# Attention's in-projection as seven block products over the whole contraction, with its weights' forms in three buffers

## What is computed

```python
def _dilated_attention_mixer(h, w_in, w_out):
    bsz, s, _ = h.shape
    proj = h @ w_in                       # (1024, 1024) @ (1024, 10240)
    qkv = proj[..., :N_DIL * 3 * A_WIDTH].reshape(bsz, s, N_DIL, 3, A_HEADS, A_HEAD_DIM)
    gate = proj[..., N_DIL * 3 * A_WIDTH:]
    for g, (window, dil) in enumerate(((128, 1), (512, 4), (2048, 16))):
        o, l = _dilated_group(qkv[:, :, g, 0], qkv[:, :, g, 1], qkv[:, :, g, 2], window, dil, slopes)
    wts = softmax(stack(lses, axis=-1))   # over the three groups
    o = einsum('bshg,bshgd->bshd', wts, stack(outs, axis=3))
    y = o.reshape(bsz, s, A_WIDTH) * silu(gate)
    return y @ w_out
```

## Time and profile before

| | |
|---|---|
| median of three runs | 2149.3 us |
| the profiled execution | 2158.68 us, span 2156.9 us |
| PE busy | 2034.0 us (94%), 10859 matmuls |
| DVE | 1306.4 us (61%) |
| ACT | 1003.0 us (47%) |
| POOL | 1062.9 us (49%) |
| DMA | 229.41 MB, 106 GB/s |
| attention's pairs | about 137 to 1154 us |

### The profile page before, as it was taken

One profiled execution on the slowest core, in us unless ns is written; L12 is line 12 of the kernel. 1 busy time (PEld: TensorE's weight loads), 2 busy tenths in 40 slices (PEclk: granted clock), 3 DMA queues, 4 the chain that ended last, 5 costly groups with the idle time before them and its releaser, 6 DMA issues.

```text
span 2156.9 us, 33831 instructions
## 1 busy us (share of the span) xinstructions
PE 2034.0 (94%) x10859; PEld 1619.4 (75%) x10859; DVE 1306.4 (61%) x2731; ACT 1003.0 (47%) x2441; POOL 1062.9 (49%) x710
## 2 busy tenths in 40 slices
PE   5799999999999999999998989899999998998997
PEld 4578787787877878878786777677777776776886
DVE  5655546446455465554555576697498498487553
ACT  3334444444434444344445245674575475485320
POOL 1533463363543635436345174475366365386572
PEclk9889999999999999999999999999999999999999
DMA  8322131221221312203024332555355355367431
GB/s 286 107 60 79 42 99 48 60 89 39 71 78 41 107 39 68 81 22 114 34 70 157 112 130 55 158 166 162 99 166 153 100 175 137 102 199 229 164 117 39
DMA packets 118408, 229.41 MB, mean 106 GB/s; under 512 B 21376, under 2 KB 64000, under 8 KB 118272
## 3 DMA queue, kind: packets, MB, share of 16 engines
q1 hardware_dynamic: 118272, 227.84, 34.3%
HBM read 199.42 MB, written 28.39 MB: 106 GB/s over the span
## 4 chain that ended last, share of the span: by engine, by line
PE 66%; DVE 13%; issue 6%; ACT 5%; DMA 4%; POOL 4%; SPq 1%; DVEq 0%; ACTq 0%; POOLq 0%
PE pp L673 18%; PE po L673 16%; PE pp_s L2369 7%; PE sp_ L750 4%; PE tp L760 3%; PE yo_p L2573 3%; DMA w_raw_s<-in_b_w 2%; DVE stage_s L2999 2%; PE po L833 2%; PE pp_s L2573 2%; DVE vv L2935 2%; PE st_p L2573 1%; PE fill L2573 1%; PE po L822 1%; ACT prob L1083 1%
## 5 line engine op out<-in xcount | busy, mean ns | idle before, releaser
L673 PE MATMUL pp<-h_forms,w_hi 128*128 128x512 f32 x1094 | 342.2, 394 | 0.0
L2369 PE MATMUL pp_s<-h_hi,w_hi_s 128*128 128x512 f32 x624 | 269.9, 433 | 22.2 <-DVE stage_s L2999 14.6
L556 POOL TENSOR_TENSOR w_lo<-w_raw,w_hi 128x1024 fp32r<-128x1024 f32 x76 | 182.8, 2406 | 218.4 <-ACT w_hi L1032 218.1
L2369 PE MATMUL pp_s<-h_hi,w_lo_s 128*128 128x512 f32 x624 | 245.9, 394 | 0.0
L2369 PE MATMUL pp_s<-h_lo,w_hi_s 128*128 128x512 f32 x624 | 245.5, 393 | 0.0
L673 PE MATMUL po<-h_forms,w_hi 128*128 128x512 f32 x760 | 238.0, 395 | 6.2 <-ACT gate L1032 6.2
L1083 ACT ACTIVATE prob<-prob,mz 128x256 f32<-128x256 f32 (+2 forms) x384 | 169.3, 442 | 140.2 <-DVE mz L1326 140.1
L673 PEld LDWEIGHTS pp<-h_forms,w_hi 128*128 128x128 f32 x1094 | 203.2, 189 | 41.0 <-ACT vT L1032 0.3
L673 PE MATMUL pp<-h_forms,w_lo 128*128 128x512 f32 x546 | 213.5, 391 | 0.0
L1346 DVE COPY probT<-tp 128x512 f32<-128x512 f32 x160 | 103.3, 684 | 134.8 <-PE tp L760 134.8
L673 PEld LDWEIGHTS po<-h_forms,w_hi 128*128 128x128 f32 x760 | 143.2, 190 | 39.9 <-ACT gate L1032 9.2
(11 more groups left out here) (524 smaller groups left out, 4594.0 us busy)
## 6 DMA issues: line engine op xcount, KB each, us to landing
w_raw<-in_a_w SPq DMA_DIRECT2D x80, 512.0 KB, 4.1
rw<-cum_rows SPq DMA_DIRECT2D x32, 1024.0 KB, 6.2
w_raw_s<-in_b_w SPq DMA_DIRECT2D x40, 512.0 KB, 3.9
ew<-exp_rows SPq DMA_DIRECT2D x64, 256.0 KB, 7.2
num_wide<-in_ada_w SPq DMA_DIRECT2D x16, 768.0 KB, 6.1
num_wide<-merge_rows SPq DMA_DIRECT2D x16, 768.0 KB, 7.8
num_wide<-in_ada_w SPq DMA_DIRECT2D x20, 512.0 KB, 6.2
yT_b<-trunk SPq DMA_DIRECT2D x32, 256.0 KB, 2.4
```

Source lines behind the costliest of these rows:

```text
L556: return nc.gpsimd.tensor_tensor(out, x, hi.bitcast(F32), ALU.subtract)
L673: last = nc.tensor.matmul(bank, w, h, start=begin and i == 0, stop=end and i == 2)
L2369: last = nc.tensor.matmul(out, w[:, slot, k, :], of_h(h, k, half), start=(k == 0 and n == 0), stop=(k == KT - 1 and n == 2))
```

## The change

All eight k tiles of every unit go through the seven products: KS is 4, PL and `plain` are gone, and so are the plainly made first tiles. A unit has seven forms of weights (B11, B21, three sums in buffers of their own, two sums in place), each of 512 elements per partition, and each form has a high and a low part in one of three buffers, `w_f[:, SLOTS[i]]`; the raw sum lies where the low part will. Forms 0, 3 and 5 share a buffer, 1 and 4, 2 and 6. h is held only in its seven forms. The first four k-tile blocks of unit 0's first three products run as h is made (`beginning`). Two units stand ahead of the pairs, every pair has five in a new order, the last pair three (d = 0 to 5). The transposes of v stand at d = 0, 3 and 8, behind the values. Buffers of the merge shrink: group 2's share is loaded when POOL has added group 1's (`third_share`), and ada_w's rows of the next layer come one by one through a ring of three, in their own pair (`NEXT_AT`), none at the start. ACT's steps are `even_step` and `odd_step`.

```diff
-KS = 2
-PL = KT - 2 * KS
+KS = KT // 2
 A11, A12, A22, S1, S2, S3, S4 = range(7)
-DUOS_OF_TILES = ((VT2, Q2), (K2, VT0), (Q0, K0), (GATE, VT1), (Q1, K1))
-LAST_DUOS = ((VT2, Q2), (K2, GATE))
-FIRST_DUO = (Q1, K1)
-PLAIN = 4
-NT_UNITS = 1 + 5 * (PAIRS - 1) + 2
-EVENTS, SUMS = 9, 9
+FIRST_DUOS = ((Q0, K0), (VT0, Q1))
+DUOS_OF_TILES = ((K1, VT1), (Q0, K2), (Q2, VT2), (K0, GATE), (VT0, Q1))
+LAST_DUOS = ((K1, VT1), (Q2, K2), (GATE, VT2))
+AHEAD = (Q0, K0, VT0, Q1)
+FIRST_UNITS = len(FIRST_DUOS)
+NT_UNITS = FIRST_UNITS + 5 * (PAIRS - 1) + len(LAST_DUOS)
+EVENTS, SUMS, FORMS = 7, 8, 7
...
+        SLOTS = (0, 1, 2, 0, 1, 0, 2)
+        PRODUCTS = (A11, A12, S3, S2, A22, S1, S4)
...
-        V_AT = {2: 2, 4: 0, 8: 1}
+        V_AT = {0: 0, 3: 1, 8: 2}
...
                 with sp.Fori(0, PAIRS - 1) as j:
-                    load_unit(5 * j + 3)
-                    store_y(j)
-                    sp.wait_ge(y_sent, 16 * j + 16)
-                    load_next(j + 1)
-                    for i in range(4, 7):
-                        load_unit(5 * j + i)
+                    n = 5 * j + 4
+                    until_next_rows(j)
+                    load_x_tile(n + 1)
+                    load_y_tile(n + 1)
+                    load_next(j, range(3, 6))
+                    load_x_tile(n + 2)
+                    load_next(j, range(6, KT))
+                    load_y_tile(n + 2)
+                    load_x_tile(n + 3)
                     stats(j, T_AT)
-                    load_unit(5 * j + 7)
+                    load_y_tile(n + 3)
                     weights_out(j)
+                    load_x_tile(n + 4)
+                    load_y_tile(n + 4)
+                    third_share(j)
...
+                def low_part(n, i, x):
+
+                    hi, lo = (w_f[:, SLOTS[i], s] for s in range(2))
+                    pool.wait_ge(w_rounded, FORMS * n + (i + 1))
+                    rest(lo, x, hi).then_inc(w_ready, 1)
+
+                def raw_form(i):
+                    return w_f_raw[:, SLOTS[i], 1]
+
+                def early_forms(n):
+
+                    first = isinstance(n, int) and n == 0
+                    low_part(n, 0, B11)
+                    low_part(n, 1, B21)
+                    pool.wait_ge(w_in[1], 16 * n + 16)
+                    if not first:
+                        pool.wait_ge(pp_full, EVENTS * n)
+                    nc.gpsimd.tensor_tensor(raw_form(2), B22, B12, ALU.subtract).then_inc(t_made, 1)
+                    pool.wait_ge(t_made, 3 * n + 1)
+                    nc.gpsimd.tensor_tensor(B12, B12, B11, ALU.subtract).then_inc(p_step, 1)
+                    low_part(n, 2, raw_form(2))
+
+                def middle_forms(n):
+
+                    pool.wait_ge(p_step, 1 if isinstance(n, int) and n == 0 else 12 + 2 * n + 1)
+                    pool.wait_ge(pp_full, EVENTS * n + 1)
+                    nc.gpsimd.tensor_tensor(raw_form(3), B22, B12, ALU.subtract).then_inc(t_made, 1)
+                    low_part(n, 3, raw_form(3))
+                    pool.wait_ge(w_ready, FORMS * n + 2)
+                    nc.gpsimd.tensor_tensor(B21, B21, B22, ALU.subtract).then_inc(p_step, 1)
+                    pool.wait_ge(p_step, 12 + 2 * n + 2)
+                    pool.wait_ge(pp_full, EVENTS * n + 2)
+                    nc.gpsimd.tensor_tensor(raw_form(4), B21, B12, ALU.add).then_inc(t_made, 1)
+                    low_part(n, 4, raw_form(4))
...
+                    n = 5 * j + 7
+                    forms(n)
+                    weigh(j, 0)
+                    weigh(j, 1)
+                    add_share(j, 1)
+                    n = 5 * j + 8
+                    early_forms(n)
+                    middle_forms(n)
+                    weigh(j, 2)
+                    low_part(n, 5, B12)
+                    add_share(j, 2)
+                    low_part(n, 6, B22)
+                    gated_sum(j)
...
+                def product(n, i, bank, blocks=range(KS)):
+
+                    (w1, w2), (h1, h2) = ([w_f[:, SLOTS[i], s] for s in range(2)],
+                                          [h[:, PRODUCTS[i]] for h in hs])
+                    for b in blocks:
+                        for t, (w, h) in enumerate(((w1, h1), (w1, h2), (w2, h1))):
+                            last = nc.tensor.matmul(bank, w[:, b], h[:, b], start=b == 0 and t == 0,
+                                                    stop=b == KS - 1 and t == 2)
+                    if blocks[-1] == KS - 1:
+                        last.then_inc(pp_full, 1)
...
                 def first_half(n):
 
-                    first = isinstance(n, int) and n == 0
-                    pe.wait_ge(w_ready, 4 * n + 1)
-                    pe.wait_ge(pp_free, PP_FREE + 4 * n - 1)
-                    product(b0, rows_of(0, B_X), A11, begin=True, end=True).then_inc(pp_full, 1)
-                    if first:
-                        pe.wait_ge(pp_free, PP_FREE)
-                    product(b1, rows_of(0, B_Y), A12, begin=True)
-                    plain(b1, 0, 0, end=True).then_inc(pp_full, 1)
-                    pe.wait_ge(w_ready, 4 * n + 2)
-                    pe.wait_ge(pp_free, PP_FREE + 4 * n)
-                    if first:
-                        pe.wait_ge(h_lo, KT + 1)
-                    product(b2, T2, S2, begin=True, end=True).then_inc(pp_full, 1)
+                    pe.wait_ge(w_ready, FORMS * n + 1)
+                    pe.wait_ge(pp_free, 4 * n - 2)
+                    product(n, 0, b0)
+                    pe.wait_ge(w_ready, FORMS * n + 2)
+                    pe.wait_ge(pp_free, 4 * n - 1)
+                    product(n, 1, b1)
+                    pe.wait_ge(w_ready, FORMS * n + 3)
+                    pe.wait_ge(pp_free, 4 * n)
+                    product(n, 2, b2)
+                    fourth_product(n)
+
+                def fourth_product(n):
+
+                    pe.wait_ge(w_ready, FORMS * n + 4)
                     pe.wait_ge(comb, SUMS * n + 1)
-                    if first:
-                        pe.wait_ge(h_lo, KT + 2)
-                    product(b0, T3, S3, begin=True, end=True).then_inc(pp_full, 1)
+                    product(n, 3, b0)
+
+                def second_half(n, between=None):
+
+                    pe.wait_ge(w_ready, FORMS * n + 5)
                     pe.wait_ge(comb, SUMS * n + 3)
-                    plain(b2, 0, 1, begin=True).then_inc(pp_full, 1)
-
-                def second_half(n, between=None):
-
-                    pe.wait_ge(w_ready, 4 * n + 4)
-                    product(b2, T4, A22, end=True).then_inc(pp_full, 1)
-                    pe.wait_ge(pp_free, PP_FREE + 4 * n + 1)
-                    if isinstance(n, int) and n == 0:
-                        pe.wait_ge(h_lo, KT + 4)
-                    product(b1, rows_of(1, B_X), S1, begin=True, end=True).then_inc(pp_full, 1)
-                    pe.wait_ge(comb, SUMS * n + 4)
-                    plain(b0, 1, 1, begin=True, end=True).then_inc(pp_full, 1)
+                    product(n, 4, b0)
+                    pe.wait_ge(w_ready, FORMS * n + 6)
+                    pe.wait_ge(pp_free, 4 * n + 1)
+                    product(n, 5, b1)
                     if between:
                         between()
-                    pe.wait_ge(pp_free, PP_FREE + 4 * n + 2)
-                    product(b2, rows_of(1, B_Y), S4, begin=True)
-                    plain(b2, 1, 0, end=True).then_inc(pp_full, 1)
+                    pe.wait_ge(w_ready, FORMS * n + 7)
+                    pe.wait_ge(comb, SUMS * n + 4)
+                    product(n, 6, b2)
...
+                pair_sums(0)
+                for i in range(KS):
+                    beginning(i, (0, 1))
+                    if i + 1 < KS:
+                        pair_sums(i + 1)
+                    beginning(i, (2,))
+                pe.wait_ge(h_lo, FORMS * KS - 1)
+                fourth_product(0)
+                pe.wait_ge(h_lo, FORMS * KS)
+                second_half(0)
+                first_half(1)
                 scores(0, 0)
-                second_half(0)
+                second_half(1)
...
-                FIRST_TILE_AT = {6: (0, 1), 7: (2, 3), 8: (4, 5, 6)}
+                FIRST_TILE_AT = {8: (0, 1, 2), 9: (3, 4, 5, 6)}
...
                 def stretch(j, d, table):
 
                     if d:
-                        new_v(j, d - 1, table)
                         duo_values(j, d - 1, table)
+                    new_v(j, d, table)
                     if d < DUOS - 1:
                         scores(j, d + 1)
                     new_probs(j, d, table)
...
+                def even_step(j, n, kinds, before, numerators_of, softmax_of):
+
+                    second_tile(j if before[1] != Q1 else j - 1, n - 1, before, 0)
+                    numerators_of()
+                    round_form(n, 2)
+                    softmax_of()
+                    round_form(n, 3)
+                    first_tile(j, n, kinds, 0)
+                    round_form(n, 4)
+
```

(47 more changed lines are left out.)

882 lines of the change are left out of this document (374 added, 508 removed).

## The result

The changed kernel takes 2163.4 us (median of four runs, 2162.0 to 2165.8), the kernel before 2149.2: a ratio of 1.0069, 95% interval 1.0051 to 1.0086. The forecast was 2105 us with a range of 2084 to 2127, so it missed by 58 us and had the wrong sign. Two runs of later experiments, of 5572 and 3330 us, lie far from the others of their kernels and are left out of the ratios.

A forecast was written before the change was run, and what follows sets the result against it. TensorE's matmul count was taken to bound the pairs, other engines being in time. Terms -31.3 + 6.2 - 6.2 + 11 - 22 - 2 = -44.3 us gave 2105 us from 2149.3, range 2084 to 2127.

The forecast's parts named there:

- Part 1: Pairs: 138 fewer matmuls at 0.227 us, -31.3 us; two more attention stretches +6.2, gate tile's wait gone -6.2.
- Part 2: Pairs: POOL, ACT and DVE bring weight forms, sums and evacuations in time despite more work; cost nothing.
- (c): Rival, pairs: fourth product late in every unit, its rounding queued behind ACT's softmaxes; 2.1 us per unit, +84, 2189 us; chance 0.05.
- Part 3: Start of each next pair: prob's transposes wait for DVE behind the shares, 1.6 us a pair, +11 us; bounds 0 and 3.
- Part 4: Start, before the loop: two units replace four plain tiles and one unit; loop begins at 115 us, -22; bounds 108 and 137.
- Part 5: End, last product to second output tile: about 36 us for 38.5, w_out's blocks through two slots; -2, bounds -9 and +4.
- The sum's carrying over to the median: Whole kernel: unprofiled median 9.4 us below the profiled execution; same difference assumed after the change, 2149.3 - 44.3 = 2105 us.
- row against rule: Start: DVE subtraction took 3.37 us beside POOL, 1.23 otherwise, agreeing that two-SBUF-input DVE and GpSimd instructions block; 22 us in full, 5 held.

The follow-up runs named there:

- the numerators in place: Changed kernel with DVE's copies first, shares behind the next duo's score maxima, and ACT copying a pair's first numerators ahead of its softmax: 2115.6 us, ratio 0.9842.
- the sums in PSUM: Changed kernel with DVE's running sums of modulation columns and gate rows at the start kept in PSUM: 2156.1 us, ratio 1.0024.
- the one experiment on them: Start's sums in PSUM, plus POOL's fourth form behind DVE's low parts, last gate rows earlier, slope's step behind the first unit's sums: 2155.3 us, ratio 1.0015.

## Why the prediction was wrong, step by step

On the profiled executions: start -8.9 us (forecast -22), pairs from the loop's first product to the last product's end +10.0 (-20.3), end +0.5 (-2), behind it +1.6 (0). Together +3.2 for -44.3; of the 47.5 us missed 30 lie in the pairs and 13 at the start.

**Part 1, matmuls: right.** 252 matmuls fewer (10607 for 10859); 0.223 to 0.229 us each by adding 96; the gate's wait gone. With the waits taken away (the numerators in place) the pairs last 982.4 us for 1017.1: -34.6, where parts 1 and 2 gave -31.3. That kernel's chain at the two ends:

```profile
126.47 5.49 PE pp L685 x24
...
1108.91 1.01 PE po L807 x8
```

**Part 2, other engines cost nothing: right for the forms, wrong as it was read.** No product waits for a form, and rival (c)'s wait appears only where an experiment delays the softmax. But the step asked only whether POOL comes in time, not whom its 203 us more of work hold up.

**Part 3, the pair's start: the step that failed.** The prediction had the wait in its place, and its slack right, but took the shares at the 2.4 us, with the bank sum, of the earlier trace rows, which were measured beside an idle POOL. The sentence that failed is "In the pairs only the weighing steps and the gate's two products are of the kind": differences and shares have two SBUF inputs as well, and POOL has forms to make there that it did not have before. The wait is 3.8 us for 1.6, outside the bounds of 0 to 3: 26.3 us in seven for 11, 15 more. And the part gave a wait no price beyond its length. The clock adds 2.2 us in the mean (1.5 to 2.6), 15.5 in seven, so that 1.6 forecast became 6.0. The two make 31 us against the 30 missed.

**Part 4, the start: mechanism right, its size wrong.** The fourth sums came at 61, as said. Of the contention, 22 us "in full", I held 5. With the sums in PSUM 9 of the 13 missed us come back, so that 14 would have been the number; the other 4 stay open, and the one experiment on them gained nothing. The fourth product was late already, 78.95 us where 73 was worked out. What was also left out of the sum is that POOL's forms of the second unit are slowed too, by the gate rows.

**Part 5, the end: inside its bounds, by another path.** 39.1 us, where about 36 was forecast, with bounds of -9 and +4 about the 38.5 before. The forecast had w_out's two slots as what sets it. In the changed kernel TensorE's long waits there are for other things, a copy of probabilities (4.0 us) and y's split (3.9); only with both moved does the chain run over the slots, and then the end lasts 34.5 us.

**The sum's carrying over to the median: wrong by 11 us.** The kernel before, profiled once more, gives the same again:

> The kernel before, unaltered, profiled once more. The profiled execution that the sum was made against took 2158.7 us, its unprofiled runs 2149.2; of the changed kernel they differ by 1 us. Theory A (that execution was by chance some 9 us long): the profile here is near 2150 us, and where it is shorter shows where the prediction's rows were long. Rival B (profiling lengthens this kernel always): near 2158 us again.

2158.70 us, after 2158.68. So that profile is hardly chance, and rival B holds: this kernel is some 9 us longer when profiled. None of the other kernels here is longer by more than 4.0, and the changed one is 1 us shorter. I had taken the same difference for both. Where in the kernel before the 9 us lie cannot be seen in a profile, and stays open.

**The rivals.** The slower one, (c), held 5% and decided by another engine's lateness; what came was the named wait of part 3 at nearly four times its price. A rival built on that wait, with the row against rule applied to it, would have been the one that ends on the other side.

## What to carry to other kernels

When a change gives an idle engine work, ask of every instruction in its new neighbourhood not only who waits for the result but who shares its way to SBUF, small instructions on the critical handover first: a duration read beside an idle neighbour is a lower bound. Count a TensorE wait of some microseconds (here 3.7) with the slow clock behind it, and look for work to put into it. Where a duration can't be protected, move the instruction behind the copies that others wait for, or the operand into PSUM.

## What the runs showed of the hardware

- A DVE operation on 32 x 64 elements, 0.21 us by itself, took up to 1.19 us beside POOL's of 1.27 us, and a POOL operation of 1.29 us took 2.28 beside DVE's gate rows. At a pair's end the long DVE operations finish within 0.25 us of POOL's: the one that comes second waits for the other's end.
- Seven idle times of TensorE of 3.7 to 3.8 us were each followed by matmuls at a granted clock of 0.50, which cost 1.5 to 1.9 us three times and 2.5 to 2.6 us four times; after idle times of 0.9 and 1.24 us it stayed at 1.00. Adding 12 matmuls in front of each wait gained 9 us in all.
- Where its loop began anew, DVE started a copy 2.2 us after the copy's input was ready (3.8 us idle), with nothing in the trace to wait for; it did so, with 3.5 to 4.4 us idle, in every turn of two kernels.
- One kernel's profiled execution was 9 us longer than its others, twice alike, the others' by at most 4.0.
